# Gated linear attention in a two-block model: the gate product in one visit on three row quarters, meta rows at full height, states two token tiles at a time

## The chip, the cores and the metric

One core of one Trainium2 chip runs the kernel. The metric is the device time of one execution in microseconds (us); a time given for a kernel is the median of its runs.

## The reference, cut to what matters

Two blocks over 528 tokens (16 meta tokens, 512 real ones) of width 1024. The first block has two layers, and each layer has a gated linear attention (GLA) of 4 heads beside a forgetting attention, then a feed-forward network. The part that the change touches:

```python
xn = rms_norm(h, attn_norm[i])
gq, gk, gv, gr, glr, fq, fk, fv, ff = jnp.split(xn @ w_in[i], cuts, axis=-1)   # glr: 16 columns, ff: 8
log_a = jax.nn.log_sigmoid(glr @ w_alpha_up[i] + b_alpha[i]) / 16.0            # 528 x 256
# chunk 0 = the 16 meta tokens, then 8 chunks of 64 tokens
log_b = jnp.cumsum(log_a, axis=3)
log_end = log_b[:, :, :, -1:, :]
u = jnp.einsum('bhntk,bhntv->bhnkv', k * jnp.exp(log_end - log_b), v)          # one 64 x 128 state increment per head
S_c = decay_c * S_{c-1} + u_c                                                  # 9 states, meta first
o_t = q_t^T S_c
```

The second block and the rest of the first are not touched.

## The kernel before, in words

Activations lie with features on partitions (`hT`, 8 tiles of 128 x 528). Every float32 product of weights and activations is made of three products of rounded parts (`wH`, `wL`, `aH`, `aL`): ScalarE (ACT) makes the high part of a weight chunk, VectorE (DVE) the low part (step `split`, L1893 and L2432), TensorE (PE) multiplies. A chunk is 128 x 1024 weights; the halves of a chunk are split apart. `wH` and `wL` hold two chunks, so chunk n+2 is split once chunk n has been multiplied.

**The order of the work is written out by hand.** `schedule()` (L300) makes one list `STEPS`, and the program of each engine runs through that list and does its part of each step, in that order. A foreground generator `fg` gives the weight products, and beside it a background generator `bg` gives the attention steps. In `run` (L431) one turn of `bg` comes after every second foreground step at this stage (`RATE_STATE` = 0.5), and a turn ends at a `yield`; steps between two yields stand in the list directly behind each other. While `bg` yields "blocked" it adds nothing.

**Foreground around the change**: `gq` (two feature-major chunks of 8 steps; matmuls of 264 columns), then token-major chunks (step `tm`, L1506; one step per token tile j, where j = 0 stands for the 16 meta rows and j = 1 to 4 for 128 tokens each): two chunks `gk` (256 columns a matmul), four `gv` and four `fv` (512 columns). The meta rows of two chunks are multiplied together in the step j = 0 of every second chunk (`meta_rows`, L1503, 16 instructions on four column tiles). The last chunk of each kind is taken out of PSUM by `tmout`: DVE takes j = 0, 1 and 3, ACT the tiles j = 2 and 4, and ACT copies three parts of the meta rows (L2025). The next kind writes to the same PSUM banks: for `gv`, tile j = 1 waits for DVE's first `tmout` of `gk` (`tm_dve`, L1526), and j = 2 for ACT's first.

**Background in each of the two layers**, in this order:
- `ffp`, `ffc`, `ffsel`: one product for the 8 `ff` and the 16 `glr` columns; `ffsel` (L1576) sums four partial rows by a matrix of ones and zeros `sel`, 128 x 48, made by POOL (GpSimd, L3168). Output rows 0 to 7 are `ff`, rows 32 to 47 are `glr`. DVE scales them out of PSUM into `ffT` and `glrT[32:48]` (`evac`, L2569), after POOL has set constants (`zeros`, L3091; semaphore `kzero`).
- `fsum`: DVE, ACT, DVE: the forget gate's log-sigmoid and its running sum.
- `gz` (L1607), three visits bk = 0, 1, 2 for the token tiles (0), (1, 2), (3, 4): PE multiplies 17 rows of `glrT` (16 and a row of ones) by `wau`, to PSUM bank bk of X; behind each visit ACT does Abs, Exp, Ln (L2237, L2239, L2241) and DVE makes `la` (L2856). bk = 0 has 16 tokens.
- `gb` (L1620), three visits: `after` (128 x 128, ones above the diagonal of each chunk) by `la`; ACT Exp (L2250), DVE scales `gk` (L2870).
- `gdec` (L1628), one visit.
- `gst` (L1637), five visits c = 0 to 4, one per token tile: 64 x 64 tiles of the array, `gk` by `gv` to X banks 0 and 1; DVE adds up the nine states `S` (L2876, L2884).
- `sums`: POOL loads rows for the forgetting attention, after all `gst`.

A float32 matmul of PE shows as two instructions (two passes) in the trace. POOL otherwise issues the DMAs that add up weight sums for the feed-forward part (`make`). SP issues the weight loads; one DMA of 34 KB loads `wau` behind the fourth of them (L3224).

In layer 0 the list around the first visits reads (chunk 3, 4 are `gk`, 5 is the first `gv`; layer 1 has the same with 157 to 159):

```
tm 3,3  split 4,1  gz 0  tm 3,4  tm 4,0  tmout 4,0  split 5,0  gz 1  tm 4,1  tmout 4,1  split 5,1
tm 4,2  tmout 4,2  gz 2  tm 4,3  tmout 4,3  tm 4,4  tmout 4,4  tm 5,0  split 6,0  tm 5,1  split 6,1  gb 0
```

Of the kernel before, what the change touches and what calls it, by code (L numbers as in the profile page):

```python
# [8 lines left out]
F32 = mybir.dt.float32  # L9
# [7 lines left out]
L = 528  # L17
# [282 lines left out]
def schedule():  # L300
# [257 lines left out]
    def attention(l):  # L558
# [64 lines left out]
        def bg():  # L623
# [3 lines left out]
            step("fsum", l)  # L627
            yield
            for bk in range(3):
                step("gz", l, bk)  # L630
                yield
            while ("gk", l) not in done:
# [6 lines left out]
            while ("gv", l) not in done:  # L639
                yield "blocked"  # L640
            for c in range(5):
                step("gst", l, c)
                yield
                yield
# [506 lines left out]
class Memory:  # L1151


    def __init__(self, nc, ctx, nvec):
# [11 lines left out]
        self.vec = sb("vec", [128, nvec])  # L1166
        self.wau = sb("wau", [49, 2, 256])
        self.rbc = sb("rbc", [128, L])
# [13 lines left out]
        self.wg = sb("wg", [128, 8, 32])  # L1182
        self.sel = sb("sel", [128, 48])
        self.G = [ctx.enter_context(nc.psum_tensor(f"G{i}", [128, 2, 512], F32)) for i in range(2)]
# [3 lines left out]
        with ExitStack() as c:  # L1188
            self.mixT = sb("mixT", [128, 8, L], F32, c)
            self.ffT = sb("ffT", [8, L], F32, c)  # L1190
            self.glrT = sb("glrT", [64, L], F32, c)
            with ExitStack() as c1:
# [153 lines left out]
def pe_program(nc, m, s):  # L1346
# [223 lines left out]
    def ffsel(l):  # L1570

        i = AT["ffglr", l]
        e.wait_ge(s.sel, 1)
        e.wait_ge(s.ffc, l + 1)
        for bank, lo, n in FULL:
            done = e.matmul(m.pair(i)[0:48, bank, 0:n], m.sel[:, :], m.osq[:, lo:lo + n], start=True, stop=True)  # L1576
        done.then_inc(s.ffsum, 1)
# [28 lines left out]

    def gz(l, bk):  # L1607
        if bk == 0:
            e.wait_ge(s.psum, NTH["evac", AT["gq", l, 1]])
            e.wait_ge(s.alpha, 16)  # L1610
        if bk == 2:
            e.wait_ge(s.rtok, RTOK["attn", l])
        mt = TOK[BLOCKS[bk][0]][1]
        for q, j in enumerate(BLOCKS[bk]):
            t0 = TOK[j][0]
            done = e.matmul(X[0:mt, bk, 256 * q:256 * q + 256], m.glrT[32:49, t0:t0 + mt], m.wau[32:49, l, :],
                            start=True, stop=True)
        done.then_inc(s.gz, 1)

    def gb(l, bk):  # L1620
        e.wait_ge(s.la, 3 * l + bk + 1)
        mt = TOK[BLOCKS[bk][0]][1]
        for q, j in enumerate(BLOCKS[bk]):
            done = e.matmul(X[0:mt, bk, 256 * q:256 * q + 256], m.after[0:mt, 0:mt], m.la[0:mt, j, :], start=True,
                            stop=True)
        done.then_inc(s.gb, 1)
# [10 lines left out]
    def gst(l, c):  # L1637


        if c == 0:  # L1640
            e.wait_ge(s.tm_act, 2 * TM_NTH["gv", l])
            e.wait_ge(s.tm_dve, 2 * TM_NTH["gv", l])
            e.wait_ge(s.tm_meta, TM_NTH["gv", l])
        else:
            e.wait_ge(s.state, 9 * l + 2 * c - 1)
        e.wait_ge(s.kd, 3 * l + (1 if c == 0 else 2 if c < 3 else 3))
        for pr in range(2):
            for hh in range(2):
                q = slice(64 * hh, 64 * hh + 64)
                for hf in range(2 if c else 1):  # L1650
                    r = slice(64 * hf, 64 * hf + 64) if c else slice(0, 16)
                    done = e.matmul(X[q, hf, 128 * pr:128 * pr + 128], m.gk[r, c, 128 * pr + 64 * hh:128 * pr + 64 * hh + 64],
                                    m.gv[r, c, 256 * pr + 128 * hh:256 * pr + 128 * hh + 128], start=True, stop=True)
                    if pr:
                        done.then_inc(s.gst, 1)

# [208 lines left out]
def act_program(nc, m, s, XT, W):  # L1865
# [363 lines left out]

    def gz(l, bk):  # L2230
# [136 lines left out]
    parts = {"high7": high7, "p1st": p1st, "p5th": p5th, "u2nd": u2nd, "c21": c21, "conv7": conv7, "silu7": silu7, "hidh7": hidh7, "split": split, "prep": prep, "xm": xm, "gains": gains, "ffc": ffc, "sq": sq, "rms": rms, "prepmid": prepmid, "last": last, "rmshalf": rmshalf, "rmsmid": rmsmid, "rmsend": rmsend, "midln": midln, "midexp": midexp,  # L2367
             "tmout": tmout, "rest": rest, "evac": evac, "mixin": mixin, "attin": attin, "gz": gz, "gb": gb, "gdec": gdec,
             "go": go, "gn": gn, "fsum": fsum, "ft": ft, "fs": fs, "fo": fo, "nsq": nsq, "nsum": nsum, "is": iscore, "dt": dt,
# [42 lines left out]
def dve_program(nc, m, s):  # L2412
# [147 lines left out]
    def evac(i):  # L2560
# [3 lines left out]
        else:  # L2564
# [4 lines left out]
            scaled(i, m.ffT[:, :], slice(0, 8)).then_inc(*own.one())  # L2569
            scaled(i, m.glrT[32:48, :], slice(32, 48)).then_inc(s.psum, 1)  # L2570
        if role[0] == "gq":
# [277 lines left out]

    def gz(l, bk):  # L2850
        n = 3 * l + bk + 1
# [20 lines left out]
    def gst(l, c):  # L2872
        e.wait_ge(s.gst, 18 * l + (4 * c + 2 if c else 2))
        if c == 0:
# [5 lines left out]
        for hf in range(2):  # L2880
            n = 2 * c - 1 + hf
            e.wait_ge(s.state, 9 * l + n)
            for pr in range(2):
                done = e.scalar_tensor_tensor(out=m.S[:, n, pr, :], in0=m.S[:, n - 1, pr, :], scalar=m.dec[:, pr, n - 1:n],  # L2884
                                              in1=X[:, hf, 128 * pr:128 * pr + 128], op0=ALU.mult, op1=ALU.add)
                if pr:
# [142 lines left out]
    def dn(n):  # L3029
# [9 lines left out]
             "rmsmid": rmsmid, "midln": midln, "rtok": rtok, "tmout": tmout, "evac": evac, "rest": rest, "normed": normed, "last": last, "store": store,  # L3039
             "pads": pads, "gz": gz, "gb": gb, "gst": gst, "gn": gn, "fsum": fsum, "fs": fs, "fmeta": fmeta, "fn": fn, "ftail": ftail,  # L3040
             "iw": iw, "is": iscore, "itri": itri, "top": top, "mask": mask, "dt": dt, "ds": ds, "dn": dn}
# [7 lines left out]
def pool_program(nc, m, s, CS, W, SU):  # L3049
# [134 lines left out]
def sp_program(nc, m, s, W, XT, MT, VE, WAU, OUT, SU):  # L3184
# [119 lines left out]
```

## Time and profile before

| | |
|---|---|
| median of 3 runs | 2253.59 us (2252.46 to 2253.8) |
| profiled execution, its own time | 2252.86 us |
| its span | 2251.6 us |
| PE busy | 2230.4 us, 99% |
| DVE, ACT, POOL busy | 63%, 47%, 5% |
| chain that ended last | PE 93%, DVE 3%, ACT 2% |
| granted PE clock | 0.999 of full speed |

"Busy" is the time in which an engine had an instruction under way. A timeline row is: start, length, engine, line, operation, output and inputs, shapes, and how many instructions are merged in it. Matmuls overlap each other, so what a matmul costs is read from the starts of the rows, not from their lengths. What a visit costs is the distance of the ordinary matmuls on both sides of it, less what they would have taken by themselves.

### The profile page before, as it was taken

Reading aid. Unit: us, or ns where it says so; the run is one execution under the profiler, and the core shown is the slowest. Engines: PE = TensorE matmul, PEld = TensorE weight load, DVE = VectorE, ACT = ScalarE, POOL = GpSimd, SP = SyncE. Lnnn points to the kernel's source line nnn. Section 1 sums busy time; section 2 is a strip of 40 time slices with the busy share of each in tenths; the row PEclk is TensorE's granted clock in tenths of the full one; section 3 lists DMA queues with packets and bytes.
Section 4 is the critical chain, followed back from the end, with each engine's and each line's share of the span. In section 5 each row is a group of like instructions: output and inputs, shape, how many; then the busy total and the mean of one; then the engine's idle time right before and its main releaser. Section 6 shows DMA issues by size and latency. Waiting matters only on the chain.

```text
span 2251.6 us, 39369 instructions
## 1 busy us (share of the span) xinstructions
PE 2230.4 (99%) x15807; PEld 2025.2 (90%) x15807; DVE 1410.6 (63%) x2601; ACT 1048.9 (47%) x1963; POOL 118.3 (5%) x203
## 2 busy tenths in 40 slices
PE   9999999999999999999999999999999999999998
PEld 7798999999997898999899888978899888998997
DVE  5356576759743465667689566869455455863664
ACT  5356554447633465544377443223244444552652
POOL 3001010000000001100000010110000000000001
PEclk9999999999999999999999999999999999999999
DMA  6555676246434435732355262777721222543651
GB/s 222 163 130 148 179 190 184 98 141 174 137 94 127 121 112 142 185 118 96 112 174 167 87 181 82 192 188 216 197 66 64 67 95 86 154 156 117 182 165 51
DMA packets 97112, 313.01 MB, mean 139 GB/s; under 512 B 13809, under 2 KB 17811, under 8 KB 95907
## 3 DMA queue, kind: packets, MB, share of 16 engines
q1 hardware_dynamic: 84627, 220.93, 30.4%
q0 software_dynamic: 11584, 88.25, 16.9%
q8 instruction: 126, 2.06, 0.4%
q10 hardware_dynamic: 720, 1.31, 0.2%
q14 instruction: 55, 0.45, 0.1%
HBM read 308.32 MB, written 86.02 MB: 175 GB/s over the span
## 4 chain that ended last, share of the span: by engine, by line
PE 93%; DVE 3%; ACT 2%; issue 1%; DMA 0%; POOL 0%; SPq 0%; ACTq 0%; DVEq 0%; POOLq 0%
PE G L1427 58%; PE G L1464 15%; PE G L1543 7%; PE X L1464 3%; PE X L1755 1%; PE X L1710 1%; PE X L1840 1%; PE X L1733 1%; DVE wL L2432 1%; PE X L1824 1%; ACT wH L1893 1%; PE X L1503 1%; PE X L1809 1%; PE X L1427 1%; PE X L1796 0%
## 5 line engine op out<-in xcount | busy, mean ns | idle before, releaser
L1893 ACT ACTIVATE wH<-raw 128x512 fp32r<-128x512 f32 (+3 forms) x693 | 475.0, 704 | 468.8 <-PE G L1427 388.5
L2432 DVE TENSOR_TENSOR wL<-raw,wH 128x512 fp32r<-128x512 f32 (+3 forms) x693 | 538.3, 788 | 238.5 <-ACT wH L1893 235.1
L1427 PE MATMUL G<-aH,wH 128*128 128x264 f32 (+2 forms) x2000 | 503.0, 316 | 2.5 <-DVE aL L2445 2.0
L1427 PE MATMUL G<-aL,wH 128*128 128x264 f32 (+2 forms) x2000 | 481.7, 306 | 0.0
L1427 PE MATMUL G<-aH,wL 128*128 128x264 f32 (+2 forms) x2000 | 481.6, 306 | 0.0
L1427 PEld LDWEIGHTS G<-aH,wH 128*128 128x128 f32 x2000 | 324.5, 189 | 28.1 <-issue 6.0
L1427 PEld LDWEIGHTS G<-aH,wL 128*128 128x128 f32 x2000 | 322.4, 188 | 17.2
L1427 PEld LDWEIGHTS G<-aL,wH 128*128 128x128 f32 x2000 | 322.9, 188 | 14.4 <-issue 0.2
L1464 PE MATMUL G<-seven,wH 128*128 128x256 f32 (+2 forms) x960 | 177.5, 284 | 1.6 <-DVE wL L2432 1.5
L2591 DVE TENSOR_TENSOR hT<-G,hT 128x528 f32<-128x528 f32 (+1 forms) x83 | 58.0, 699 | 183.0 <-PE G L1427 183.0
L1464 PEld LDWEIGHTS G<-seven,wH 128*128 128x128 f32 x960 | 148.1, 188 | 3.7 <-issue 2.9
L1427 PE MATMUL G<-hidH,wH 128*128 128x264 f32 (+1 forms) x528 | 140.4, 320 | 0.7 <-DVE hidL L2678 0.7
L1427 PE MATMUL G<-hidL,wH 128*128 128x264 f32 (+1 forms) x528 | 141.1, 321 | 0.0
L1427 PE MATMUL G<-hidH,wL 128*128 128x264 f32 (+1 forms) x528 | 140.8, 321 | 0.0
L1464 PE MATMUL G<-aH,wH 128*128 128x256 f32 (+2 forms) x480 | 136.5, 284 | 1.0 <-ACT G L2161 1.0
L1464 PE MATMUL G<-aL,wH 128*128 128x256 f32 (+2 forms) x480 | 135.5, 282 | 0.0
L1464 PE MATMUL G<-seven,wL 128*128 128x256 f32 (+2 forms) x480 | 135.4, 282 | 0.0
L1464 PE MATMUL G<-aH,wL 128*128 128x256 f32 (+2 forms) x480 | 135.4, 282 | 0.0
L1543 PE MATMUL G<-wH,aH 128*128 128x512 f32 (+1 forms) x256 | 97.7, 382 | 0.4 <-DVE wL L2432 0.4
L1427 PEld LDWEIGHTS G<-hidH,wH 128*128 128x128 f32 x528 | 87.4, 188 | 9.7 <-DVE hidL L2678 1.4
L1427 PEld LDWEIGHTS G<-hidH,wL 128*128 128x128 f32 x528 | 87.7, 188 | 7.5
L1427 PEld LDWEIGHTS G<-hidL,wH 128*128 128x128 f32 x528 | 87.5, 188 | 7.6
(407 smaller groups left out, 3911.0 us busy)
## 6 DMA issues: line engine op xcount, KB each, us to landing
raw<-weights SPq DMA_DIRECT2D x195, 512.0 KB, 3.8
weight_sums<-weights POOLq DMA_DIRECT2D x72, 704.0 KB, 6.4
raw<-weight_sums SPq DMA_DIRECT2D x160, 256.0 KB, 2.9
raw<-weights SPq DMA_DIRECT2D x48, 704.0 KB, 4.1
raw<-weights SPq DMA_DIRECT2D x121, 256.0 KB, 2.9
weight_sums<-weight_sums POOLq DMA_DIRECT2D x24, 704.0 KB, 5.2
weight_sums<-weights POOLq DMA_DIRECT2D x24, 448.0 KB, 4.9
raw<-weights SPq DMA_DIRECT2D x12, 384.0 KB, 5.4
```

The lines of the kernel that those rows point to most:

```text
L1427: done = e.matmul(m.pair(i)[0:M, bank, 0:n], a[:, k, 0:M], b[:, kx, lo - t0:lo - t0 + n], start=(k == 0 and c == 0), stop=(k == nk - 1 and ...
L1464: done = e.matmul(out, a[:, k, :], b[:, k, :], start=(p in (1, 2, 5) and k == 0 and c == 0), stop=(k == 3 and c == 2), skip_group_check=p ...
L1503: e.matmul(out[32 * t:32 * t + 32, 0:256], m.xm[:, c * nk + kk, :], wr[:, kk, 256 * half:256 * half + 256], start=(c == 0), stop=(c == 8 / ...
L1543: done = e.matmul(out[:, 0:cols], a[:, k, t0:t0 + 128], b[:, kk, :], start=(k == 0 and q == 0), stop=(k == 7 and q == 2))
L1710: e.matmul(X[:, hh, at:at + nk], a[r, p % 2, tq:tq + 128], k[r, p % 2, lo:lo + nk], start=(c == at == 0), stop=(c == 2 and at == 400), ski ...
L1733: done = e.transpose(X[:, 2, 128 * q:128 * q + 128], m.Sb[:, 2 * (n % 2) + hh, at:at + 128], m.ident[:, :])
L1755: done = e.matmul(X[64 * hh:64 * hh + 64, 3, at:at + nq], m.fv[:, j, c:c + 64], m.PT[:, 2 * (n % 2) + hh, t, 0:nq], start=first, stop=last)
L1809: done = e.transpose(o, m.Sb2[b][:, TOK[j][0]:TOK[j][0] + 128], m.ident[:, :])
L1824: done = e.matmul(X[:, bank, 0:nn], a[:, hb, 128 * i:128 * i + 128], k[:, hb, lo:lo + nn], start=(c == 0), stop=(c == 2))
L1893: e.activation(m.high(i)[:, c], m.raw(i)[:, c], ACT.Copy).then_inc(s.w_hi, 1)
L2432: e.tensor_tensor(m.low(i)[:, c], m.raw(i)[:, c], m.high(i)[:, c].bitcast(F32), ALU.subtract).then_inc(s.w_lo, 1)
L2591: e.tensor_tensor(h, m.psum(i), h, ALU.add).then_inc(s.psum, 1)
```

## The change

The gate product is issued in one visit. `glr` is now made on three groups of 16 rows (`sel` has 112 columns), scaled into `glrT[32:48]`, `[64:80]` and `[96:112]`, each with a row of ones behind it, and `wau` is loaded three times, so that the matmuls of X banks 0, 1, 2 read rows 96, 32 and 64 on. All of them use 128 tokens, tile 0 too. The ACT and DVE part is a step of its own (`gla`), three times directly behind each other at the next turn. `gb` bk = 0 and `gst` c = 0 work on 128 and 64 rows instead of 16; POOL zeroes the unused rows of `la`, `gk` and `gv`. `gst` has three visits: tiles 0 and 1, tiles 2 and 3, tile 4, with three turns each; odd tiles write the second half of the banks.

```diff
@@ schedule(), attention, bg
+            step("gz", l)
+            yield
             for bk in range(3):
-                step("gz", l, bk)
-                yield
+                step("gla", l, bk)
             while ("gk", l) not in done:
                 yield "blocked"
...
-            for c in range(5):
+            for c in (0, 2, 4):
                 step("gst", l, c)
+                yield
                 yield
                 yield
@@ PE, ffsel
-            done = e.matmul(m.pair(i)[0:48, bank, 0:n], m.sel[:, :], ...)
+            done = e.matmul(m.pair(i)[0:112, bank, 0:n], m.sel[:, :], ...)
@@ PE, gz
+        e.wait_ge(s.psum, NTH["evac", AT["gq", l, 1]])
+        e.wait_ge(s.alpha, 48)
+        e.wait_ge(s.rtok, RTOK["attn", l])
+        e.wait_ge(s.kzero, l + 1)
+        for bk, q in (0, 0), (1, 0), (2, 0), (1, 1), (2, 1):
+            t0, g = TOK[BLOCKS[bk][q]][0], (96, 32, 64)[bk]
+            done = e.matmul(X[:, bk, 256 * q:256 * q + 256], m.glrT[g:g + 17, t0:t0 + 128], m.wau[g:g + 17, l, :], ...)
+            if q == len(BLOCKS[bk]) - 1:
+                done.then_inc(s.gz, 1)
@@ PE, gb
-            done = e.matmul(X[0:mt, bk, 256 * q:256 * q + 256], m.after[0:mt, 0:mt], m.la[0:mt, j, :], ...)
+            done = e.matmul(X[:, bk, 256 * q:256 * q + 256], m.after[:, :], m.la[:, j, :], ...)
@@ PE, gst
+            e.wait_ge(s.kd, 3 * l + 2)            # c == 0; otherwise state 9l+2c-1 and kd 3l+3
...
+        for d in range(c, min(c + 2, 5)):
+            ...
+                        r, at = slice(64 * hf, 64 * hf + 64), 256 * (d % 2) + 128 * pr
@@ DVE, evac of ffglr
-            scaled(i, m.glrT[32:48, :], slice(32, 48)).then_inc(s.psum, 1)
+            for g in (32, 64):
+                scaled(i, m.glrT[g:g + 16, :], slice(g, g + 16)).then_inc(*own.one())
+            scaled(i, m.glrT[96:112, :], slice(96, 112)).then_inc(s.psum, 1)
@@ POOL, zeros
         constant(m.glrT[32:64, :], 1.0)
+        constant(m.glrT[64:128, :], 1.0)
+        for t in m.la, m.gk, m.gv:
+            constant(t[:, 0, :], 0.0)
@@ POOL, sel
-        for c, n, row in (0, 8, 0), (32, 16, 8):
+        for c, n, row in (0, 8, 0), (32, 16, 8), (64, 16, 8), (96, 16, 8):
@@ SP
-    e.dma_start(m.wau[32:49, :, :], WAU.rearrange("l r n -> r l n")).then_inc(s.alpha, 16)
+    for g in (32, 64, 96):
+        e.dma_start(m.wau[g:g + 17, :, :], WAU.rearrange("l r n -> r l n")).then_inc(s.alpha, 16)
```

## Rows read from the trace of the kernel before

**Rows 1.** The page: busy time, share of the span, instructions, of PE.

```profile
PE 2230.4 (99%) x15807; PEld 2025.2 (90%) x15807; DVE 1410.6 (63%) x2601; ACT 1048.9 (47%) x1963; POOL 118.3 (5%) x203
```

**Rows 2.** Timeline of PE, layer 1, around the norm's sums and `ffsel`.

```profile
662.67 0.61 PE L1585 MATMUL X<-tmpn,ones 128*128 128x264 f32 x2
...
663.80 0.40 PE L1427 MATMUL G<-aL,wH 128*128 128x264 f32 x2
...
664.77 0.41 PE L1427 MATMUL X<-aH,wL 128*128 128x264 f32 x2
665.11 1.09 PE L1576 MATMUL G<-osq,sel 128*48 128x264 f32 x4
...
666.48 0.40 PE L1427 MATMUL X<-aL,wH 128*128 128x264 f32 x2
```

**Rows 3.** Timeline of PE, layer 1, the three `gz` visits and the first `gv` matmul.

```profile
676.85 0.60 PE L1616 MATMUL X<-wau,glrT 17*16 17x256 f32 x2
...
677.60 0.28 PE L1543 MATMUL G<-wH,aL 128*128 128x256 f32 x1
...
680.00 1.13 PE L1616 MATMUL X<-wau,glrT 17*128 17x256 f32 x4
681.05 0.39 PE L1543 MATMUL G<-wH,aH 128*128 128x256 f32 x1
...
684.08 1.12 PE L1616 MATMUL X<-wau,glrT 17*128 17x256 f32 x4
...
685.36 0.28 PE L1543 MATMUL G<-wH,aL 128*128 128x256 f32 x1
...
688.09 0.39 PE L1543 MATMUL G<-wH,aH 128*128 128x512 f32 x1
```

**Rows 4.** Timeline of PE, layer 1, `gb` of the meta rows.

```profile
689.58 0.60 PE L1624 MATMUL X<-la,after 16*16 16x256 f32 x2
...
690.45 0.39 PE L1543 MATMUL G<-wH,aL 128*128 128x512 f32 x1
```

**Rows 5.** Timeline of PE, layer 0, two of the `gst` visits.

```profile
78.38 0.67 PE L1652 MATMUL X<-gv,gk 64*64 64x128 f32 x16
78.98 0.50 PE L1543 MATMUL G<-wH,aH 128*128 128x512 f32 x1
...
84.75 0.67 PE L1652 MATMUL X<-gv,gk 64*64 64x128 f32 x16
...
85.69 0.39 PE L1543 MATMUL G<-wH,aL 128*128 128x512 f32 x1
```

**Rows 6.** Windows, layer 1: length; busy PE, PEld, DVE, ACT, POOL; PEclk; DMA.

```profile
677.48:678.81 1.33, 1.33 (x12) 1.33 (x12) 1.33 (x2) 1.26 (x3) 0.00 (x0) 1.00 0.00 0
680.26:682.39 2.13, 2.13 (x15) 1.74 (x15) 0.53 (x2) 2.03 (x5) 0.00 (x0) 1.00 1.07 342
682.39:684.32 1.93, 1.93 (x16) 1.79 (x16) 1.37 (x3) 1.86 (x4) 0.00 (x0) 1.00 0.53 210
```

**Rows 7.** Timeline of DVE, layer 1, behind the second gate block.

```profile
684.44 0.69 DVE L2856 SCALAR_TENSOR_TENSOR la<-X,S 128x512 f32<-128x512 f32 x1 [0.65 <-ACT S L2241]
685.05 0.47 DVE L2548 TENSOR_SCALAR gk<-G,rtok 128x256 f32<-128x256 f32 x1
```

**Rows 8.** Timeline of POOL, layer 0: `sel` and the last of `zeros`.

```profile
6.36 3.80 POOL L3168 TENSOR_SCALAR_AFFINE_SELECT sel<-sel 32x8 f32<-32x8 f32 x8
...
16.60 0.53 POOL L3097 MEMSET fv<- 128x512 f32 x1
```

**Rows 9.** Timeline of DVE, layer 0: scaling `glr` out of PSUM.

```profile
25.69 0.70 DVE L2557 TENSOR_TENSOR glrT<-G,rbc 16x528 f32<-16x528 f32 x1
```

**Rows 10.** Windows at the end of the program, columns as in rows 6.

```profile
2244.00:2246.00 2.00, 0.70 (x2) 0.30 (x2) 1.46 (x5) 1.14 (x3) 1.54 (x2) 1.00 0.61 207
2246.00:2248.00 2.00, 0.00 (x0) 0.00 (x0) 2.00 (x6) 0.05 (x1) 1.64 (x2) 0.89 0.79 266
```

**Rows 11.** Timeline of PE, first matmuls of the program.

```profile
1.58 5.46 PE L1847 MATMUL X<-ident 128*128 128x128 f32 x32 [1.58 <-POOL ident L3144]
```

More of the change, by code:

```diff
@@ L1166, in __init__ @@
         self.vec = sb("vec", [128, nvec])
-        self.wau = sb("wau", [49, 2, 256])
+        self.wau = sb("wau", [113, 2, 256])
         self.rbc = sb("rbc", [128, L])
@@ L1182, in __init__ @@
         self.wg = sb("wg", [128, 8, 32])
-        self.sel = sb("sel", [128, 48])
+        self.sel = sb("sel", [128, 112])
         self.G = [ctx.enter_context(nc.psum_tensor(f"G{i}", [128, 2, 512], F32)) for i in range(2)]
@@ L1190, in __init__ @@
             self.ffT = sb("ffT", [8, L], F32, c)
-            self.glrT = sb("glrT", [64, L], F32, c)
+            self.glrT = sb("glrT", [128, L], F32, c)
             with ExitStack() as c1:
@@ L1575, in ffsel @@
         for bank, lo, n in FULL:
-            done = e.matmul(m.pair(i)[0:48, bank, 0:n], m.sel[:, :], m.osq[:, lo:lo + n], start=True, stop=True)
+            done = e.matmul(m.pair(i)[0:112, bank, 0:n], m.sel[:, :], m.osq[:, lo:lo + n], start=True, stop=True)
         done.then_inc(s.ffsum, 1)
@@ L1605, in pe_program, with gz @@
     BLOCKS = ((0,), (1, 2), (3, 4))
[L1607 to L1616, printed above, removed]
+    def gz(l):
+        e.wait_ge(s.psum, NTH["evac", AT["gq", l, 1]])
[4 more added lines that the diff above has]
+            t0, g = TOK[BLOCKS[bk][q]][0], (96, 32, 64)[bk]
+            done = e.matmul(X[:, bk, 256 * q:256 * q + 256], m.glrT[g:g + 17, t0:t0 + 128], m.wau[g:g + 17, l, :],
                             start=True, stop=True)
-        done.then_inc(s.gz, 1)
+            if q == len(BLOCKS[bk]) - 1:
+                done.then_inc(s.gz, 1)
     def gb(l, bk):
         e.wait_ge(s.la, 3 * l + bk + 1)
-        mt = TOK[BLOCKS[bk][0]][1]
         for q, j in enumerate(BLOCKS[bk]):
-            done = e.matmul(X[0:mt, bk, 256 * q:256 * q + 256], m.after[0:mt, 0:mt], m.la[0:mt, j, :], start=True,
-                            stop=True)
+            done = e.matmul(X[:, bk, 256 * q:256 * q + 256], m.after[:, :], m.la[:, j, :], start=True, stop=True)
         done.then_inc(s.gb, 1)
@@ L1643, in gst @@
             e.wait_ge(s.tm_meta, TM_NTH["gv", l])
+            e.wait_ge(s.kd, 3 * l + 2)
         else:
             e.wait_ge(s.state, 9 * l + 2 * c - 1)
[L1646 to L1655, printed above, removed]
+            e.wait_ge(s.kd, 3 * l + 3)
+        for d in range(c, min(c + 2, 5)):
+            for pr in range(2):
+                for hh in range(2):
+                    q = slice(64 * hh, 64 * hh + 64)
+                    for hf in range(2 if d else 1):
+                        r, at = slice(64 * hf, 64 * hf + 64), 256 * (d % 2) + 128 * pr
+                        done = e.matmul(X[q, hf, at:at + 128], m.gk[r, d, 128 * pr + 64 * hh:128 * pr + 64 * hh + 64],
+                                        m.gv[r, d, 256 * pr + 128 * hh:256 * pr + 128 * hh + 128], start=True, stop=True)
+                        if pr:
+                            done.then_inc(s.gst, 1)
     def go(l, v):
@@ L2227, in attin, with gla @@
         operand_high(m.q2H[:, h, :] if h < 2 else m.aH[:, h, NM:L], m.attnT[:, h, :], 1.0)
-    def gz(l, bk):
+    def gla(l, bk):
         n = 3 * l + bk + 1
@@ L2367, in act_program @@
     parts = {"high7": high7, "p1st": p1st, "p5th": p5th, "u2nd": u2nd, "c21": c21, "conv7": conv7, "silu7": silu7, "hidh7": hidh7, "split": split, "prep": prep, "xm": xm, "gains": gains, "ffc": ffc, "sq": sq, "rms": rms, "prepmid": prepmid, "last": last, "rmshalf": rmshalf, "rmsmid": rmsmid, "rmsend": rmsend, "midln": midln, "midexp": midexp,
-             "tmout": tmout, "rest": rest, "evac": evac, "mixin": mixin, "attin": attin, "gz": gz, "gb": gb, "gdec": gdec,
+             "tmout": tmout, "rest": rest, "evac": evac, "mixin": mixin, "attin": attin, "gla": gla, "gb": gb, "gdec": gdec,
              "go": go, "gn": gn, "fsum": fsum, "ft": ft, "fs": fs, "fo": fo, "nsq": nsq, "nsum": nsum, "is": iscore, "dt": dt,
@@ L2847, in pads, with gla @@
         e.memset(m.Hs[:, :, 0:2], 0.0).then_inc(*own.one())
-    def gz(l, bk):
+    def gla(l, bk):
         n = 3 * l + bk + 1
@@ L2872, in gst, with state @@
     def gst(l, c):
-        e.wait_ge(s.gst, 18 * l + (4 * c + 2 if c else 2))
+        end = min(c + 2, 5)
+        e.wait_ge(s.gst, 18 * l + 4 * end - 2)
+        for d in range(c, end):
+            state(l, d)
+    def state(l, c):
         if c == 0:
@@ L2884, in gst @@
                 done = e.scalar_tensor_tensor(out=m.S[:, n, pr, :], in0=m.S[:, n - 1, pr, :], scalar=m.dec[:, pr, n - 1:n],
-                                              in1=X[:, hf, 128 * pr:128 * pr + 128], op0=ALU.mult, op1=ALU.add)
+                                              in1=X[:, hf, 256 * (c % 2) + 128 * pr:256 * (c % 2) + 128 * pr + 128], op0=ALU.mult,
+                                              op1=ALU.add)
                 if pr:
@@ L3039, in dve_program @@
              "rmsmid": rmsmid, "midln": midln, "rtok": rtok, "tmout": tmout, "evac": evac, "rest": rest, "normed": normed, "last": last, "store": store,
-             "pads": pads, "gz": gz, "gb": gb, "gst": gst, "gn": gn, "fsum": fsum, "fs": fs, "fmeta": fmeta, "fn": fn, "ftail": ftail,
+             "pads": pads, "gla": gla, "gb": gb, "gst": gst, "gn": gn, "fsum": fsum, "fs": fs, "fmeta": fmeta, "fn": fn, "ftail": ftail,
              "iw": iw, "is": iscore, "itri": itri, "top": top, "mask": mask, "dt": dt, "ds": ds, "dn": dn}
@@ L3169, in pool_program @@
                                    compare_op=ALU.not_equal, fill=1.0, base=-row, pattern=[[-1, n]], channel_multiplier=1)
-            if (t, c) == (3, 32):
+            if (t, c) == (3, 96):
                 done.then_inc(s.sel, 1)
```

## The prediction, made before the changed kernel was run

> **What bounds the kernel now.** I read the page first. PE is busy for 2230.4 of 2251.6 us [rows 1], and it waits for next to nothing between its first and last work, so a stage is worth what it takes on PE's line of time, or the wait that it makes there. Then I read PE's timeline around each step of the diff, in both layers (the two show the same distances to 0.01 us, so one layer's rows stand for both), and after that the timelines of ACT, DVE and POOL, for what PE would wait for if it came earlier. Changes under 0.2% (4.5 us) can't be told from none.
>
> How a visit is priced: 23 matmuls of 256 columns lie between 685.36 and 688.09, 0.12 us each [rows 3]; four pairs of 264 columns between 663.80 and 664.77, 0.12 each [rows 2]; six of 512 columns lead from 688.09 to the visit at 689.58, 0.23 each and 0.10 more [rows 3, 4]. Those 0.09 to 0.10 stand ahead of each visit whose tile is smaller than 128 x 128: 0.34 from a pair that takes 0.24 to `ffsel` [rows 2]. Ahead of L1585, with full tiles, nothing does. The price is this lead, and the distance from the visit's start to the second ordinary matmul behind it, less one ordinary step.
>
> **The change part by part, per layer.**
>
> `ffsel` goes from 48 to 112 columns. L1576 costs 0.09 + 1.37 - 0.24 = 1.22 us; the norm's four full-tile passes of the same 264 columns cost 1.13 - 0.24 = 0.89, 0.22 a pass [rows 2]. The difference is the change of tile size and back. With 112 columns it should be a full tile like L1585: 0.33 saved (bounds 0 and 0.33).
>
> `gz`. The three visits cost 0.09 + 0.75 - 0.12 = 0.72, 1.05 (behind the meta rows' visit) and 0.09 + 1.28 - 0.12 = 1.25: 3.02 us [rows 3]. The new visit has ten passes of 256 columns on three quarters, at most four on one. If quarters run side by side it is as long as the last old visit, with four passes: 1.25. If they don't, six passes of 0.22 more: 2.57. Nearest are the 64 x 64 tiles of `gst`, where 16 passes of 128 columns leave after 0.60 us [rows 5], which one after the other at half of 0.22 would take 1.8; so I take 1.25. It can't be below the four passes, 0.88. Saved on PE: 1.77.
>
> By the Trainium skill (TensorE: Matmul & The Clock Gate, the section on packing small matmuls) four row tiles gave 3.07 times one, not four times. No row here has quarters. By it I estimate four rounds at 1.3 times their length, 0.26 us more a layer, and the sum below would be 0.5 us higher.
>
> `gb` of the meta rows costs 0.10 + 0.87 - 0.23 = 0.74 [rows 4]; with full tiles, two passes at 0.22: 0.44. Saved 0.30.
>
> `gst`. An isolated visit costs 0.10 + 0.94 - 0.23 = 0.81, one behind the meta rows 0.60 [rows 5]. Four rounds of passes at 0.11 are in each, so 0.37 is the switch (0.16 where it is joined). Before: four isolated and one joined, 3.84. After: the same 20 rounds (the meta tile's passes keep two tiles busy, and use the same rows as half of tile 1) in three isolated visits, 20 x 0.11 + 3 x 0.37 = 3.31. Saved 0.53. `go` comes at the same turn: five visits with two turns are ten, three with three are nine, and the tenth passes while `fv` isn't done. The longer bursts on DVE lie between splits.
>
> PE has 0.33 + 1.77 + 0.30 + 0.53 = 2.93 us less to do per layer, 5.9 in both.
>
> **What is late next: the gate's ACT and DVE part.** Before, its three blocks stood at three turns, with the evacuation of `gk` and the splits between them. Now `gla` 0, 1 and 2 stand behind each other at the second turn, after `split 5,0` and ahead of `tmout 4,1`, DVE's first evacuation of `gk`, without which `gv`'s first matmul may not write its bank; behind it stands `split 5,1`, which that tile needs in its second half. ACT and DVE go in order, so PE gets there only when all three blocks are through. For layer 1: the meta rows' visit moves by -0.33 (`ffsel`) and +0.53 (1.25 for 0.72), so ACT's copies start at 680.26 + 0.20 = 680.46. Copies and a split take 2.13 [rows 6], the meta block 1.33, the second 1.93, so the third starts at 685.85. DVE's `la` follows 2.05 after its start (684.44 against 682.39), and `tmout` 0.61 after that and is 0.47 long [rows 6, 7]: 688.98, and PE about 0.07 later, by estimate, at 689.05. Before, that matmul started at 688.09 [rows 3]; with the savings PE could be there at 688.09 - 0.33 - 1.77 = 685.99. It waits 3.06 us. The saving of 2.10 turns into a loss of 0.96. (`split 5,1` is ready 0.1 us before it is wanted.)
>
> **Hidden parts.** DVE scales `glr` three times, 2 x 0.7 us more [rows 9]. In layer 0 that delays the scaling of `gq` and `rtok` behind it by 1.4 us, which the `gz` visit still finds done, and `split 4,1` by as much, to within a few tenths of need; what it might cost there shortens the later wait, since ACT and DVE set that one. POOL has 8 more selects (3.80 for 8) and four more memsets, each taken as long as the 0.53 of `fv` and 0.07 between them: `kzero` moves from 17.1 to at most 23.3 [rows 8]; DVE needs it ahead of `ffT`, 0.7 before 25.69 [rows 9], so 1.7 us of slack. If that were gone, DVE would be late by it and PE with it. In layer 1 only the memsets come. The first sums of weights on POOL start up to 6 us later, which no PE wait hangs on. SP issues two more DMAs of 34 KB behind the first four weight loads; the loads behind them are for chunks that are split only once earlier ones have been multiplied. The full height of `la`, `gk` and `gv` costs no engine an instruction.
>
> **Sum.** Per layer +0.96 - 0.30 - 0.53 = +0.13; in both +0.3. The profiled execution (2252.86 us, 0.73 under the median) would become 2253.1, the median 2253.59 + 0.3 = 2253.9.
>
> **The rivals.**
>
> A, no wait in the way: if `gv` doesn't wait for the gate blocks (ACT and DVE much quicker back to back than apart, or the banks free earlier), all 5.9 us are kept: 2247.7, faster by 0.26%. Against it: the blocks' durations are measured, and the order of the steps is fixed. A wait shorter by half gives 2250.8.
>
> B, the quarters run one after another: 2.57 for 1.25, and the ACT chain starts that much later: +1.3 per layer, 2256.5. Also the case in which the visit doesn't do what it says. The bank order (each quarter has its own) and the side-by-side 64 x 64 tiles speak against it.
>
> C, slower by the clock. After PE's last matmul the granted clock fell within 2246 to 2248 us; 0.89 in that stretch puts the fall at 2247.6, at most 2.9 us after PE's last work, the 0.70 us in the two before it [rows 10]. So from an idle PE the clock can fall to its lower level (1.2 instead of 2.4 GHz) within about the 3.06 us that I forecast. The price is read at the start: 32 passes of 128 columns took 5.46 us [rows 11] where at 0.11 they would take 3.5, so 2.0 us a fall. In both layers: 2253.9 + 4.0 = 2257.9, slower by 0.19%; if the return takes twice as long, 2261.9. It decides from the point at which the wait is as long as the one at the end, near 3 us.
>
> The page on the clock gate has the rule that speaks against this change: the Trainium skill (TensorE: Matmul & The Clock Gate, section on why this matters) wants no long idle gaps between bursts of matmuls, since the array then falls back to half rate. The row at the end agrees; the middle of this program shows no gap of such length.
>
> **How the numbers follow.** My forecast has 0.62, A 0.14 (half of it with part of the wait), B 0.07, C 0.17. The forecast's own range is 2252.6 to 2255.2 (0.3 us either way in each layer's chain, the skill's 0.5, a late POOL). The range asked for, 2249.5 to 2258.5, leaves out full A and the worse half of C. Faster by over 0.2% is full A and a little: 0.12. Slower by over 0.2% (above 2258.1) is C with a slow return, or B and C together: 0.11. The rest, 0.77, is the same.
>
> **What would show it.** In the profile after: one L1616 group a layer, about 1.1 us to the next matmul, starts in threes; L1576 with no lead; three groups of L1652, the first with 24 instructions. PE idle of about 3 us ahead of the first `gv` matmul in both layers, released by DVE's `gk` scaling or the split behind it, in layer 1 near 689.0 us; PE's idle time up by 6. ACT's nine gate operations without a pause. The forecast is wrong if this idle is under 2 us, if the granted clock leaves 1.00 behind it, or if new waits stand elsewhere.

## The result, and the profile after

The changed kernel takes **2256.6 us** (median of 22 runs, 2254.91 to 2258.78) against 2253.38 us before (22 runs, 2252.46 to 2254.03) in the same comparison: ratio 1.0016, 95% interval 1.0009 to 1.0023. It is slower by 0.16%: the interval lies above 1, so the difference is real, but it is less than the 0.2% from which the prediction counts a change, and so by that measure the time is the same. Its runs lie over 3.9 us, those of before over 1.6.

The page of the changed kernel, one execution of 2256.25 us, set against [rows 1]; the last line is the granted clock in 40 slices of the span:

```profile
span 2255.0 us, 39395 instructions
...
PE 2228.1 (99%) x15807; PEld 2027.3 (90%) x15807; DVE 1413.8 (63%) x2605; ACT 1048.5 (46%) x1963; POOL 128.7 (6%) x219
...
PEclk9999999999999999999999999999999999999999
```

PE has 2.3 us less busy time and the span is 3.4 us longer: PE waits for 5.7 us more. The view of PE's waits over the whole program names them (line, releaser: sum, times, longest), and PE's timeline places them; the visits of the diff stand between:

```profile
PE G L1545 <- DVE gk L2550: 4.8, 2, 3.0
...
PE G L1545 <- DVE wL L2434: 1.3, 2, 0.9
```

```profile
30.11 0.39 PE L1545 MATMUL G<-wH,aH 128*128 128x256 f32 x1 [0.78 <-DVE glrT L2559]
...
37.34 0.39 PE L1545 MATMUL G<-wH,aH 128*128 128x256 f32 x1 [0.92 <-DVE wL L2434]
...
44.39 0.47 PE L1545 MATMUL G<-wH,aH 128*128 128x512 f32 x1 [1.84 <-DVE gk L2550]
...
76.11 1.09 PE L1654 MATMUL X<-gv,gk 64*64 64x128 f32 x24
77.13 0.50 PE L1545 MATMUL G<-wH,aH 128*128 128x512 f32 x1
...
667.58 0.41 PE L1429 MATMUL X<-aH,wL 128*128 128x264 f32 x2
667.83 1.05 PE L1578 MATMUL G<-osq,sel 128*112 128x264 f32 x4
668.52 0.60 PE L1429 MATMUL X<-aH,wH 128*128 128x264 f32 x2
...
679.32 1.14 PE L1617 MATMUL X<-wau,glrT 17*128 17x256 f32 x10
...
691.95 0.47 PE L1545 MATMUL G<-wH,aH 128*128 128x512 f32 x1 [2.98 <-DVE gk L2550]
...
693.42 0.59 PE L1625 MATMUL X<-la,after 128*128 128x256 f32 x2
693.66 0.58 PE L1545 MATMUL G<-wH,aH 128*128 128x512 f32 x1
```

What these rows show: `ffsel` follows its pair after 0.25 us, with no lead, where before 0.34 lay ahead of it [rows 2]; one `gz` visit of ten passes [rows 3]; `gb` of the meta rows without a lead [rows 4]; and the first `gv` matmul, 688.09 before [rows 3], behind a wait of 2.98 us. The two short waits at 30.11 and 37.34 us are in layer 0 alone.

What ends the long wait stands on ACT's and DVE's timelines, layer 1:

```profile
685.41 0.37 ACT L2239 ACTIVATE S<-X 16x256 f32<-16x256 f32 x1
...
686.69 0.57 ACT L2239 ACTIVATE S<-X 128x512 f32<-128x512 f32 x1
...
688.58 0.58 ACT L2239 ACTIVATE S<-X 128x512 f32<-128x512 f32 x1
...
689.86 0.72 ACT L2243 ACTIVATE S<-S,ones 128x512 f32<-128x512 f32 x1
```

```profile
690.61 0.69 DVE L2860 SCALAR_TENSOR_TENSOR la<-X,S 128x512 f32<-128x512 f32 x1 [1.21 <-ACT S L2243]
691.22 0.47 DVE L2550 TENSOR_SCALAR gk<-G,rtok 128x256 f32<-128x256 f32 x1
```

Nine gate operations of ACT without a pause, DVE's `la` of the third block waiting for the last of them, and `gk`'s scaling behind it.

**Where the time went.** Both traces hold the same 13185 instructions of PE that read `wH` or `wL`, in the same order, so the start of each in one timeline can be subtracted from its start in the other (matched starts). How much later (+) or earlier (-) PE comes than before, by part, in us:

| | layer 0 | layer 1 |
|---|---|---|
| `ffsel` | -0.33 | -0.33 |
| `gz`: +0.54 - 1.06 - 1.14 - 0.11 | -1.77 | -1.77 |
| the two short waits, with their edges | +2.0 | none |
| behind the meta rows' visit (34.44), in every run with the change | +0.2 | none |
| the long wait | +2.0 | +3.14 |
| the first `gv` matmul's own step, 0.30 for 0.23 | +0.08 | +0.09 |
| `gb` | -0.30 | -0.30 |
| `gst` | -0.52 | -0.52 |
| **behind the long wait, where no wait explains it** | **+1.6** | none |
| together | +3.0 | +0.3 |

The long wait is shorter in layer 0 because PE comes late to it already. Another 0.2 us stand ahead of 15 us, 0.4 come back between the layers, and behind layer 1 the two timelines keep their distance to 0.3 us up to the end. Windows of PE (length, busy, granted clock, DMA) show what the 1.6 us are:

```profile
44.00:46.00 2.00, 1.61 (x6) 0.82 1.05 360
46.00:48.00 2.00, 2.00 (x6) 0.50 0.01 4
48.00:50.00 2.00, 2.00 (x9) 0.82 0.16 17
```

The granted clock was 0.50, its lower level (1.2 GHz), from 46 to 48 us and for part of the windows on both sides: it fell once, after the wait that ended at 44.39, and came back before 50 us. In layer 1 of this execution it stayed at full speed behind a longer wait.

### The profile page after: what moved, and what is told of

It is laid out like the page before. It is cut to its first block, busy times and chain, and to the rows that moved or that the text cites. A ratio compares the mean times of both kernels' runs of the same rounds, so it can differ in the third digit from the quotient of the medians.

```text
span 2255.0 us, 39395 instructions
## 1 busy us (share of the span) xinstructions
PE 2228.1 (99%) x15807; PEld 2027.3 (90%) x15807; DVE 1413.8 (63%) x2605; ACT 1048.5 (46%) x1963; POOL 128.7 (6%) x219
## 4 chain that ended last, share of the span: by engine, by line
PE 91%; DVE 4%; ACT 3%; issue 1%; POOL 1%; POOLq 0%; ACTq 0%; DVEq 0%
PE G L1429 58%; PE G L1466 15%; PE G L1545 6%; PE X L1466 3%; PE X L1757 1%; PE X L1712 1%; PE X L1842 1%; PE X L1735 1%; DVE wL L2434 1%; PE X L1826 1%; ACT wH L1895 1%; PE X L1811 1%; PE X L1505 1%; PE X L1798 0%; PE X L1671 0%
## 5 line engine op out<-in xcount | busy, mean ns | idle before, releaser
L1429 PE MATMUL G<-aH,wH 128*128 128x264 f32 (+2 forms) x2000 | 502.5, 316 | 1.6 <-DVE aL L2447 1.1
L1429 PE MATMUL G<-aH,wL 128*128 128x264 f32 (+2 forms) x2000 | 481.7, 306 | 0.0
L1429 PE MATMUL G<-aL,wH 128*128 128x264 f32 (+2 forms) x2000 | 481.3, 306 | 0.0
L1429 PEld LDWEIGHTS G<-aH,wH 128*128 128x128 f32 x2000 | 324.6, 189 | 27.0 <-issue 5.3
L1429 PEld LDWEIGHTS G<-aH,wL 128*128 128x128 f32 x2000 | 322.6, 188 | 17.2
L1429 PEld LDWEIGHTS G<-aL,wH 128*128 128x128 f32 x2000 | 322.7, 188 | 14.4 <-issue 0.2
L1466 PE MATMUL G<-seven,wH 128*128 128x256 f32 (+2 forms) x960 | 177.5, 284 | 1.6 <-DVE wL L2434 1.5
L1466 PEld LDWEIGHTS G<-seven,wH 128*128 128x128 f32 x960 | 148.0, 188 | 3.8 <-issue 3.0
L1429 PE MATMUL G<-hidH,wH 128*128 128x264 f32 (+1 forms) x528 | 140.5, 321 | 0.7 <-DVE hidL L2682 0.7
L1429 PE MATMUL G<-hidL,wH 128*128 128x264 f32 (+1 forms) x528 | 141.1, 321 | 0.0
L1429 PE MATMUL G<-hidH,wL 128*128 128x264 f32 (+1 forms) x528 | 140.9, 321 | 0.0
L1466 PE MATMUL G<-aH,wH 128*128 128x256 f32 (+2 forms) x480 | 136.6, 285 | 1.0 <-ACT G L2163 1.0
L1466 PE MATMUL G<-aL,wH 128*128 128x256 f32 (+2 forms) x480 | 135.5, 282 | 0.0
L1466 PE MATMUL G<-aH,wL 128*128 128x256 f32 (+2 forms) x480 | 135.4, 282 | 0.0
L1466 PE MATMUL G<-seven,wL 128*128 128x256 f32 (+2 forms) x480 | 135.4, 282 | 0.0
L1429 PEld LDWEIGHTS G<-hidH,wH 128*128 128x128 f32 x528 | 87.4, 188 | 9.6 <-DVE hidL L2682 1.3
L1429 PEld LDWEIGHTS G<-hidL,wH 128*128 128x128 f32 x528 | 87.5, 188 | 7.7
L1429 PEld LDWEIGHTS G<-hidH,wL 128*128 128x128 f32 x528 | 87.7, 188 | 7.5
```

The lines of the kernel that those rows point to most:

```text
L1429: done = e.matmul(m.pair(i)[0:M, bank, 0:n], a[:, k, 0:M], b[:, kx, lo - t0:lo - t0 + n], start=(k == 0 and c == 0), stop=(k == nk - 1 and ...
L1466: done = e.matmul(out, a[:, k, :], b[:, k, :], start=(p in (1, 2, 5) and k == 0 and c == 0), stop=(k == 3 and c == 2), skip_group_check=p ...
```

## The experiments

Three theories stood after this. First, the blocks of the gate back to back make the wait that eats the saving. Second, POOL's late zeroing makes the two short waits. Third, the clock falls behind the long wait, in some executions in no layer, in others in one or both. The first four runs take one edit for each, and the first two together. The kernel before was measured again beside each group of runs: 2253.72 us beside the first four, 2253.61 beside the next four, 2253.89 beside the last two, where it had been 2253.38 beside the changed kernel. So a difference between runs of two groups is good to about 0.3 us.

**Blocks apart.** The ACT and DVE parts go back to three turns, the first in the turn of the new PE visit. The edit does two things: it spreads the blocks, and it starts the first of them one turn earlier than in the changed kernel:

```diff
             step("gz", l)
-            yield
             for bk in range(3):
                 step("gla", l, bk)
+                yield
```

> The changed kernel with one edit: the three gate blocks of ACT and DVE are given at three turns again, the first with the new PE visit, as the kernel before gave them. If the wait ahead of the first gv matmul comes from their standing back to back ahead of DVE's gk scaling (first theory), it is gone in both layers (under 0.3 us instead of 1.84 and 2.98), and the time is 2253.4 - 5.9 = 2247.5 us, or up to 1.7 more for what POOL's late zeroing costs in layer 0 (0.78 and 0.92 us of PE waits): 2247.5 to 2249.3. No fall of the clock in the layers, and runs as close together as before's (2252.5 to 2254.0 there). If the expected saving on PE was never there (rival), a wait or none, the time stays at 2254 or more; if ACT's and DVE's chain is simply too long wherever its blocks stand, the wait moves to the first gb visit and the time is within 1 us of 2256.6.

Measured: **2249.92 us** (11 runs, 2249.54 to 2250.22), before 2253.72, ratio 0.9983 (0.9974 to 0.9992). The long wait is gone in both layers; `gk`'s first scaling now stands behind the second block's `la` and ahead of the third's, and PE's timeline shows the first `gv` matmul 6.45 us earlier than in the changed kernel, with no wait ahead of it:

```profile
685.50 0.47 PE L1545 MATMUL G<-wH,aH 128*128 128x512 f32 x1
```

```profile
684.15 0.69 DVE L2860 SCALAR_TENSOR_TENSOR la<-X,S 128x512 f32<-128x512 f32 x1 [0.65 <-ACT S L2243]
684.76 0.48 DVE L2550 TENSOR_SCALAR gk<-G,rtok 128x256 f32<-128x256 f32 x1
...
686.94 0.69 DVE L2860 SCALAR_TENSOR_TENSOR la<-X,S 128x512 f32<-128x512 f32 x1 [1.10 <-ACT S L2243]
```

In layer 1 the stage gains 2.85 us on before by matched starts; 2.93 were forecast for the work alone. Layer 0 gains only about 1.1: waits of 1.0 and 0.3 us remain, the POOL part. The rival that the chain would hold up `gb` instead falls: no wait stands there. Whether the earlier start alone would do, with the blocks still together, was not tried.

**Fewer selects on POOL.** One select over a pattern with a step of 32 writes the three copies of 16 columns; `sel` becomes 128 wide for it:

```diff
-        self.sel = sb("sel", [128, 112])
+        self.sel = sb("sel", [128, 128])
...
-        for c, n, row in (0, 8, 0), (32, 16, 8), (64, 16, 8), (96, 16, 8):
+        for c in (0, 32):
+            part = m.sel[32 * t:32 * t + 32, 0:8] if c == 0 else \
+                m.sel[32 * t:32 * t + 32, 32:128].rearrange("p (g n) -> p g n", n=32)[:, :, 0:16]
```

> The changed kernel with one edit: the 16 selects of POOL become 8, the three copies of the 16 columns written by one select over a pattern with a step of 32. Second theory: POOL's zeroing, late at 27.0 us in layer 0, held DVE for 1.90 us and PE for 0.78 and 0.92 us; with about 4.5 us less of selects it is done at 22 to 23 us, ahead of DVE's need at about 25, both PE waits go, and the time falls by 1.0 to 1.7 us to 2254.9 to 2255.6. The wait ahead of the gv matmul stays at 3 us in layer 1 and grows to as much in layer 0 at most. Rival: the two PE waits only trade places with the one at gv, since ACT's chain sets the end; then the time stays within 0.4 us of 2256.6.

Measured: 2254.13 us (11 runs, 2252.91 to 2255.16), ratio 1.0001 (0.9993 to 1.0010). The two short waits are gone, as expected, and the wait at `gv` in layer 0 grew from 1.84 to 2.80, since PE now came to it earlier. But the sum did not fit: 2.5 us less than the changed kernel, of which the matched starts put only a part in the gate. From 1935 us on, far behind anything that the edit touches, the matmuls of the program's last feed-forward network ran quicker. So a fourth theory was needed.

**Both edits.**

> Both edits together. If the two theories hold, nothing of the PE saving is lost: 2253.4 - 5.9 = 2247.5 us, ratio to the kernel before 0.9974, runs within 1.6 us of each other. If the late zeroing is hidden once the blocks stand apart, it equals the run with the blocks apart alone.

Measured: **2245.3 us** (5 runs, 2245.28 to 2245.99), ratio **0.9963** (0.9950 to 0.9975): 8.4 us under before, faster than both kernels, and 2.5 us more than the whole saving forecast on PE. No wait of PE is left in the two gate stages. By matched starts the two stages gain 2.74 and 2.87 us; 3.1 us more are gained behind 1935 us.

**PE kept busy in the wait.** Matmuls of `ident` into a free bank, whose result is not used:

```diff
+                if name == "gv" and j == 1:
+                    for _ in range(20):
+                        e.matmul(X[:, 3, 0:128], m.ident[:, :], m.ident[:, :], start=True, stop=True)
```

> The changed kernel with PE busy in the wait: 20 matmuls of 128 x 128 into a bank that is free, ahead of the wait of the first gv matmul; their results are not used. They take 20 x 0.11 = 2.2 us of the 3.0 us of wait. Third theory: the clock fell behind this wait once in the profiled run (3.4 us at half speed) and none, once or twice in others, 1.7 us each; with PE busy it does not fall, the wait of PE ends at the same moment, the time is 2256.6 - 1.7 = 2254.9 us and the runs lie as close together as the quickest of the changed kernel, 2254.9 to 2255.5. Rival: the fall costs nothing that counts (ACT and DVE set the pace behind it); then the time stays at 2256.6. If the fillers delay the gv matmul instead (layer 0, where the wait is only 1.84), up to 0.4 us are given back.

Measured: 2258.87 us (11 runs, 2257.72 to 2259.24): more, where 2254.9 was expected: the price of the fillers was wrong. Twenty matmuls are forty passes, which took 4.6 us and pushed the `gv` matmul back:

```profile
41.99 4.63 PE L1526 MATMUL X<-ident 128*128 128x128 f32 x40
46.37 0.48 PE L1548 MATMUL G<-wH,aH 128*128 128x512 f32 x1
```

The mean clock was 0.999 in all 11 runs, so none shows a fall, but what that saved can't be told from what the fillers cost. So the next run has eight.

**Eight instead of twenty** (`range(8)`; the expectation speaks of the run above).

> As the run with 20 matmuls of filling, with 8: each of those was two passes of 0.11 us, so 20 took 4.4 us where the wait was 3.0 and 1.84, and pushed the gv matmul back by 1.3 and 2.5. Eight take 1.8 us and fit into both waits. Third theory: the clock does not fall behind a wait that is cut to 0.1 and 1.2 us; the time is that of the changed kernel without its falls, 2256.6 - 1.7 = 2254.9 us, and the runs lie within 1.2 us of each other where those of the changed kernel spread over 3.9. If the clock has no part in it, 2256.6.

Measured: **2254.8 us** (11 runs, 2254.17 to 2255.11), ratio 1.0004 (0.9995 to 1.0013), 1.8 us under the changed kernel, with a spread of 0.9 us where that one had 3.9, and with a mean clock of 0.999 in all 11 runs. PE's timeline and windows:

```profile
42.51 1.95 PE L1526 MATMUL X<-ident 128*128 128x128 f32 x16
44.33 0.47 PE L1548 MATMUL G<-wH,aH 128*128 128x512 f32 x1
```

```profile
44.00:46.00 2.00, 2.00 (x12) 1.00 1.18 365
46.00:48.00 2.00, 2.00 (x10) 1.00 0.00 0
```

The `gv` matmul starts where it did (44.33 for 44.39), the clock stays at 1.00, and the 1.6 us behind it are gone. The two short waits are still there (0.8 and 0.9 us), so it is the wait at `gv` that brings the clock down. The falls cost the changed kernel 1.8 us in the median (2.0 when each is set against its own measurement of before).

**The place in memory alone.** The changed kernel, and the kernel before, with nothing but a wider `sel`, so that all behind it moves by 64 bytes:

```diff
-        self.sel = sb("sel", [128, 112])
+        self.sel = sb("sel", [128, 128])
```

> The changed kernel with sel allocated 128 columns wide instead of 112 (the extra 16 are never read), and nothing else: all that lies behind it in SBUF moves by 64 bytes. In the two runs with this width the matmuls L1429 of the second feed-forward layer's seven-products took 0.1145 us a step instead of 0.1194, from about 1935 us on, and these runs gained 2.7 to 2.9 us there. If the place in memory does that (fourth theory), this kernel is 2.7 us under the changed one, 2253.9 us, with the same gain in the same stretch; then the run with 8 selects (2254.13) owed its gain to this and POOL's late zeroing cost next to nothing while the gate blocks stand back to back. If it comes from POOL's selects or the program's length, the time stays at 2256.6.

> The kernel before with sel allocated 64 columns wide instead of 48, nothing else. Fourth theory: a shift of 64 bytes alone gives the same 2.7 us as in the two others: 2253.7 - 2.7 = 2251.0 us, ratio 0.9988. If the gain belongs to the absolute place (320 bytes further in the others than in the kernel before), or to the change, it stays at 2253.7.

(The line meant there is L1466, L1464 before, and the feed-forward network is the last of three; L1429 and "second" were slips.) Measured: 2253.56 us (11 runs, 2251.68 to 2255.61) for 2256.6, and **2250.58 us** (11 runs, 2250.35 to 2251.37) for 2253.61, ratio 0.9987 (0.9979 to 0.9996): 3.0 us each time for 64 bytes that nobody reads. By matched starts it is 3.1 us behind 1935 us in both. PE's groups by form, 1935 to 2000 us, of before and of before with the wider `sel`, whose last number ahead of the second bar is the mean of one:

```profile
L1464 PE MATMUL G<-seven,wH 128*128 128x256 f32 x168 | 30.7, 283 | 0.2 <-DVE wL L2432 0.2
L1464 PE MATMUL G<-seven,wL 128*128 128x256 f32 x84 | 23.6, 281 | 0.0
```

```profile
L1464 PE MATMUL G<-seven,wH 128*128 128x256 f32 x168 | 29.7, 279 | 0.2 <-DVE wL L2432 0.2
L1464 PE MATMUL G<-seven,wL 128*128 128x256 f32 x84 | 23.3, 277 | 0.0
```

Start to start it is 0.1196 against 0.1150 us a pass. The change itself moves what lies behind `sel` by 256 bytes, and there the same groups keep 282 and 281 ns, and from 1000 us to the end the changed kernel's distance to before stays within 0.3 us: the place played next to no part in its result.

**Blocks apart, with the place moved but all 16 selects.**

> The gate blocks apart and sel 128 columns wide, with all 16 selects of POOL. Against the run with the blocks apart alone (2249.92) it shows the place in memory: 2247.2 us by the fourth theory. Against the run with both edits (2245.3) it shows POOL's late zeroing alone: by the second theory, which the traces of those two put at 1.6 us up to the end of layer 0's gate, 2245.3 + 1.6 = 2246.9 us. If both hold the two sums agree to 0.3 us; if the 8 selects gave the 2.7 us and not the width, it is 2249.9.

Measured: **2247.06 us** (6 runs, 2246.88 to 2247.19), ratio 0.9971 (0.9959 to 0.9982). Both expected sums hold to 0.2 us: 2249.92 - 2247.06 = 2.9 us for the place, 2247.06 - 2245.3 = 1.8 us for POOL's late zeroing. With the blocks back to back eight selects less gained nothing in the median: 2253.56 with 16, 2254.13 with 8. There POOL's delay shortened a wait that came later (1.84 for 2.80 us); with the short waits gone PE had two long ones, and the clock two places to fall. The runs' mean clocks fit that: with 16 selects three of 11 runs kept 0.999 (2251.68, 2252.05, 2252.16 us), with 8 none did. That the clock falls more often behind a longer wait is argued from these, not shown. The quickest runs with 8, 2252.91 to 2253.69 at 0.998, would by estimate be at 2251.3 to 2252.1 without a fall of 1.6, hardly under the three with 16.

**Two more places**, both edits with `sel` 144 and 160 wide:

> The run with both edits (2245.3) with sel 144 columns wide instead of 128, so that all behind it lies 64 bytes further, 384 from the kernel before. Where the place counted so far, 0 and 256 bytes gave the slow matmuls in the last products (0.1194 us a step) and 64 and 320 the quick ones (0.1145). If the place repeats with 256 bytes, this is an untried one: if only the first 64 of 256 were the bad one, the time stays at 2245.3; if the quick one is the exception, it returns to 2245.3 + 2.7 = 2248.0.

> The same with sel 160 columns wide, 448 bytes from the kernel before. As there: 2245.3 if all places but 0 and 256 are quick, 2248.0 if 64 and 320 alone are. If the time goes another way in the two, the matmuls' pace depends on how their two operands lie to each other's reads and writes, and each product should show its own step.

Measured: 2248.18 us (9 runs) and 2247.2 us (7 runs), against 2245.3 with 128. Not one good and one bad place: with 144 the passes of `seven` take 0.1203 us from start to start (with 128: 0.1150), but those of `hid2` (512 columns) 0.227 instead of 0.233; 160 lies between. Of the places tried the two products have different best ones; why the place matters was not tried.

## Why the prediction was right, and where only by luck

**Right, by its steps.** The visits cost what was read from the rows: matched starts give `gz` 1.77 us less (forecast 1.77), `ffsel` 0.33 (0.33), `gst` 0.52 (0.53), `gb` 0.30 (0.30). Not in the forecast are 0.08 us that the first `gv` matmul takes longer to the next in every run with the change; no run explains them. The quarters run side by side: L1617, ten passes, reaches the next work in about 1.1 us, so rival B falls. The Trainium skill (TensorE: Matmul & The Clock Gate, the section on packing small matmuls) gives four row tiles 3.07 times one; the trace does not show that loss with three. The wait was there, released as said: 2.98 us in layer 1 for 3.06. It ended at 691.95, and since everything reaches layer 1 2.80 us late, that is 689.15 for the forecast 689.05. Blocks apart shows that this wait, with the fall of the clock behind it, ate the saving: 6.7 us come back by moving three steps, of which about 1.8 are the clock.

**Wrong in POOL's bound.** "`kzero` moves from 17.1 to at most 23.3" failed: it came at 27.0, and the 1.7 us of slack were gone. Two of the prediction's own signs of being wrong came of it: new waits elsewhere (0.78 and 0.92 us), and in layer 0 a long wait of 1.84 us, under the 2 that it asked for. POOL's timeline after, and with 8 selects and blocks apart:

```profile
6.44 9.51 POOL L3181 TENSOR_SCALAR_AFFINE_SELECT sel<-sel 32x8 f32<-32x8 f32 x16
16.04 7.87 POOL L3084 TENSOR_SCALAR xm<-hT,vec 128x32 f32<-128x32 f32 x8
...
26.49 0.53 POOL L3110 MEMSET fv<- 128x512 f32 x1
```

```profile
6.42 4.16 POOL L3183 TENSOR_SCALAR_AFFINE_SELECT sel<-sel 32x8 f32<-32x8 f32 x8
10.68 5.69 POOL L3084 TENSOR_SCALAR xm<-hT,vec 128x32 f32<-128x32 f32 x8
...
18.95 0.53 POOL L3110 MEMSET fv<- 128x512 f32 x1
```

The step priced the added selects at the mean of the old ones (7.6 us for 16; they took 9.51) and left `xm` as it was. But a POOL operation that reads SBUF was longer here beside some of DVE's work (the rows are in the last section), and a later start puts it beside other work: the eight `xm` took 5.7 us when they began at 10.7 and 7.9 when they began at 16.0. DVE then waited until 27.15:

```profile
27.15 0.70 DVE L2559 TENSOR_TENSOR ffT<-G,rbc 8x528 f32<-8x528 f32 x1 [1.90 <-POOL fv L3110]
```

The price is 1.8 us where nothing hides it (both edits against blocks apart at the same place), and here about 0.9 by estimate: 2.0 us of waits, less the 1.1 by which the long wait was shorter.

**Wrong in the choice between forecast and rival C.** The forecast held the clock at 1.00 behind the wait and said that leaving it would prove it wrong. It left it, at least once in 20 of 22 runs by their mean clock (0.998 or 0.997; two runs at 0.999, as in all 38 runs with the blocks apart). The times stand in groups: two runs up to 2255.1 without a fall, 12 from 2255.7 to 2256.9, eight from 2257.7 on; that these are one and two falls is argued from their distance. Rival C had the mechanism and nearly the price (2.0 us a fall, measured 1.6). Its point of decision, "near 3 us", was too high: the clock fell behind a wait of 1.84. And it was taken as both layers or none, while a fall comes behind some of these waits and not behind others. The Trainium skill (TensorE: Matmul & The Clock Gate, section on why this matters) asks for no long idle gaps of PE between bursts of matmuls. The trace agrees in kind and goes further: 1.6 us were lost behind a wait of 1.84, shorter than the gap that the page warns of, and none behind one of 2.98 in the same execution.

**The sum.** 2253.4 before, + 0.3 forecast, + 0.9 POOL, + 1.8 clock = 2256.4, measured 2256.6. The run with eight fillers, where only the clock is mended, bears out the first three: 1.2 us over its own measurement of before. The other way round, both edits: 8.4 us, less 2.9 for the place, leaves 5.5 of the 5.9 forecast for PE's work (5.6 by matched starts). The forecast's own range, 2252.6 to 2255.2, missed it by 1.4 us; the wide range and the verdict "the same" held because the errors are small against the 0.2%, not because every term was right. There is luck in it: both errors went the same way, and the five runs from 2258.54 to 2258.78 lie outside even the wide range. Had the clock fallen behind both waits in most runs, as rival C has it, the median would be near them.

## What to carry to other kernels

Price a visit by lead and distance, then ask which in-order engine has to be through what before PE's next bank is free: three blocks given at one turn turned 5.9 us of saving into a loss of 3.2, and given at three turns they leave a gain of 3.8. Here a wait of 1.8 to 3.0 us on PE cost itself and, in most runs, a fall of the clock of 1.6 us; the spread of the runs (3.9 us for 0.9) was the sign. When a kernel is measured to a tenth of a per cent, compare at the same place in memory: pad so that what lies behind keeps its address, or test the padding by itself.

## What the runs showed of the hardware that was not expected

**POOL beside DVE.** A select of 32 x 16 takes 190 ns with DVE idle (9.2 to 10.1 us; one of the three is 32 x 8) and 574 while DVE runs its operation on three inputs (6.9 to 8.7 us); an `xm` of 128 x 32 takes over 1.0 us beside DVE's squares (18.2 to 20.8 us). Groups of POOL in these windows, mean ns ahead of the second bar:

```profile
L3181 POOL TENSOR_SCALAR_AFFINE_SELECT sel<-sel 32x16 f32<-32x16 f32 x3 | 1.7, 574 | 0.4
```

```profile
L3181 POOL TENSOR_SCALAR_AFFINE_SELECT sel<-sel 32x16 f32<-32x16 f32 (+1 forms) x3 | 0.6, 190 | 0.4
```

```profile
L3084 POOL TENSOR_SCALAR xm<-hT,vec 128x32 f32<-128x32 f32 x3 | 3.2, 1063 | 0.3
```

Memsets, which read nothing, keep 0.53 us for 512 columns with DVE idle (at 26.49) and beside DVE's squares (at 18.95 with 8 selects). The Trainium skill (SBUF — State Buffer, the section on the two separate sides) has GpSimd operations that read SBUF and DVE operations with two SBUF inputs take turns, each for a whole instruction. The rows agree as far as they go: what reads SBUF is longer beside such DVE operations (574 for 190 ns), and the memsets are not.

**64 bytes of SBUF are 3.0 us.** The place of the operands changes the pace of dense matmuls by 4% (0.1196 to 0.1150 us a pass of 256 columns), in the last feed-forward network; in the two before it, with the same lines of code, the same 64 bytes moved the sum by 0.3 us or less. Between them and the last one the matched starts of before with the wider `sel` gain 1.0 us from 1530 to 1620 and lose 1.3 from 1840 to 1900, so one padding has stages of both signs and only the sum shows in the time.

**The length of the wait does not settle whether the clock falls.** Behind waits of nearly the same length (2.80 us in layer 0 and 2.99 in layer 1 of the run with 8 selects) the granted clock stayed at 1.00 in the first case and was 0.61 and 0.54 in the two stretches of 2 us behind the second:

```profile
44.00:46.00 2.00, 2.00 (x10) 1.00 0.13 49
46.00:48.00 2.00, 2.00 (x10) 1.00 0.00 0
...
690.00:692.00 2.00, 1.89 (x5) 0.61 0.00 0
692.00:694.00 2.00, 2.00 (x6) 0.54 1.06 360
```

The kernel before, which has no such wait, showed a mean clock of 0.998 in one of 28 runs too (2255.33 us).
